# Hybrid decoder step: the first 384 tokens of the u projection from x before its norm, with the norm's inverse root applied at eviction, first weights in halves, and 48 TensorE products of zeros at the start

## The chip, the cores and the metric

The kernel runs on one core of a Trainium2 chip. The metric is the device time of one execution in microseconds (us), the median of three runs for the kernel before. The engines are TensorE (PE, with PEld for its weight loads), VectorE (DVE), ScalarE (ACT), GpSimd (POOL) and SyncE (SP), which only issues DMAs; ACT and POOL issue DMAs too.

## The reference

One layer of a decoder with three token mixers, for 1024 prompt tokens and 32 sample tokens together (1056 columns). What the change touches is the norm in front of the combined projection and the first columns of that projection, u, which feed the S5 mixer:

```python
def rmsnorm(x, w):
    xf = x.astype(jnp.float32)
    y = xf * lax.rsqrt(jnp.mean(xf * xf, axis=-1, keepdims=True) + EPS)
    return (y * w.astype(jnp.float32)).astype(x.dtype)
...
    h = rmsnorm(x, norm1_w)
    proj = h @ w_in
...
    y_b, s5_new = s5_mixer(proj[..., OFF_U:OFF_Q], ...)
```

The inverse root is one number for each token. It can be applied to h before the product, or to the product of (x times the norm's weight) behind it: the result is the same sum.

## The kernel before

Tokens lie along the free dimension, channels on the 128 partitions: x is eight tiles (k = 0 to 7) of 128 channels by 1056 tokens. The tokens are worked in three chunks, 0 and 1 of 384 and 2 of 288 columns. Every product is made of three TensorE products of 128 by 128 weights: operands are split into a high part (HH of the activations, WH of the weights) and a low part (HL, WL), and `mm3` multiplies HL by WH, HH by WL and HH by WH into one PSUM bank. Each engine runs its list of instructions in order; semaphores join them.

The u projection has four output tiles (j = 0 to 3), each with weights of 1024 columns. Units 0 and 1 of the weights go into WH and WL, units 2 and 3 into WXH and WXL. TensorE works `u_pair(j, n)`: tiles j and j+1 of chunk n, over all eight k, 48 products. The order is pairs (0, 0) and (2, 0), then the same two for chunk 1 and for chunk 2.

Ahead of each chunk stands its norm. ACT and DVE square x and DVE adds the eight squares; TensorE sums over partitions (`x_sums_pe`), ACT takes the root (`x_root_act`), DVE the reciprocal (`x_recip_dve`), and TensorE spreads it over partitions (`x_spread_pe`). Then, for each k, `x_split_dve` makes the normed row on DVE (line 702), ACT rounds it to HH (line 714), and DVE subtracts to get HL (line 691). The sums and the spread of chunks 1 and 2 are put between products of the second pair of the chunk ahead, behind k = 1 and k = 3. ACT evicts the products of u to UF (line 2398).

High parts of weights are made by ACT (lines 2355, 2344, 2348), low parts by POOL (lines 1496 and 1487). Behind chunk 2 the gates begin: `gate(0)` needs unit 4 of the weights (high part by ACT in `high_weights`, low part by POOL) in WH slot 0. `taps(0)`, two thirds into gate 0 (behind its chunks 0 and 1), needs the S5 matrices W_re and W_im, which DVE makes in six operations of 2048 columns right behind the last split of the 24. POOL makes the powers they need (`s5_powers`, `s5_rows`).

SP issues, in this order, chunk 0 of x, two small tables (HOT, RTAB), weights 0, 1 and 2, chunk 1 of x, weights 3, chunk 2 of x and the rest. ACT issues one DMA, the parameters.

Of the kernel before, what the change touches and what calls it, by code (L numbers as in the profile page):

```python
# [9 lines left out]
F32 = mybir.dt.float32  # L10
# [146 lines left out]
def build(nc, io):  # L157
# [255 lines left out]
    s_xc = [dma_sem("x_chunk1_first"), dma_sem("x_chunk1_last"), dma_sem("x_chunk2")]  # L413
# [6 lines left out]
    first_high, half_ok = sem("first_weights_high"), sem("first_weights_half_split")  # L420
    s_rawx = [dma_sem(f"weights_second_pair{i}") for i in range(2)]
# [57 lines left out]
    h_lo_pool = sem("h_low_by_pool")  # L479
# [127 lines left out]
    def x_spread_at(n):  # L607

        return bank[(4, 7, 5)[n]]

    def x_full(i):

        return bank[5 + i % 2] if i < KD else HF[i % 2]

    def x_loaded(n, k):

        return s_x[k] if n == 0 else s_xc[k // 4] if n == 1 else s_xc[2]

    def x_first_square(eng, k):

        eng.wait_ge(x_loaded(0, k), 16)
        if k % 2 == 0:
            nc.scalar.activation(x_square_at(0, k), X0[:, k, 0:384], ACT.Square).then_inc(pq_done, 1)
        else:
            nc.vector.tensor_tensor(x_square_at(0, k), X0[:, k, 0:384], X0[:, k, 0:384], ALU.mult).then_inc(pq_used, 1)

    def x_squares_act(n, ks):
        c0, w = CHUNKS[n]
        base = FIRST_ADDED + KD * (n - 1)
        for k in ks:  # L630
            nc.scalar.wait_ge(x_loaded(n, k), (16, 64, 128)[n])
            if k >= 4 or n == 2:
                nc.scalar.wait_ge(pq_used, base + k - 3)
            nc.scalar.activation(x_square_at(n, k), X0[:, k, c0:c0 + w], ACT.Square).then_inc(pq_done, 1)

    def x_add_dve(n, ks):
        dve = nc.vector
        c0, w = CHUNKS[n]
        for k in ks:
            i = FIRST_ADDED + KD * (n - 1) + k  # L640
            dve.wait_ge(pq_done, FIRST_SQUARES + KD * (n - 1) + k + 1)
            if k == 0:
                dve.tensor_copy(ACC[:, c0:c0 + w], x_square_at(n, k)).then_inc(pq_used, 1)
            else:
                dve.wait_ge(pq_used, i)
                dve.tensor_tensor(ACC[:, c0:c0 + w], ACC[:, c0:c0 + w], x_square_at(n, k), ALU.add).then_inc(pq_used, 1)

    def x_first_sums_pe():

        for k, added in ((1, 2), (3, 4), (7, FIRST_ADDED)):  # L650
            nc.tensor.wait_ge(pq_used, added)
            for j in range(3):
                last = nc.tensor.matmul(x_sums_at(0)[:, j:j + 1], x_square_at(0, k)[:, P * j:P * j + P], prm("ones", 0, 1),
                                        start=(k == 1 and j == 0), stop=k == KD - 1, skip_group_check=True)
# [3155 lines left out]
```

## Time and profile before

| | us |
|---|---|
| median of 3 runs | 1686.33 |
| lowest and highest | 1684.88, 1686.92 |
| span of the profiled execution | 1684.5 |
| TensorE busy in it | 1654.0 (98%) |
| DVE, POOL, ACT busy | 966.9, 791.2, 556.0 |
| first product of u | 17.30 |
| first product of gate 0 | 69.16 |
| first product of taps(0) | 77.89 |

TensorE works without a break from 17.30 us on but for some short waits, so its few idle pieces, and the rate of its products where the clock is low, make up what is not work. What lies between two products of one engine is read from the start of one to the start of the next, since their records overlap.

### The profile page before, as it was taken

Reading aid. Unit: us, or ns where it says so; the run is one execution under the profiler, and the core shown is the slowest. Engines: PE = TensorE matmul, PEld = TensorE weight load, DVE = VectorE, ACT = ScalarE, POOL = GpSimd, SP = SyncE. Lnnn points to the kernel's source line nnn. Section 1 sums busy time; section 2 is a strip of 40 time slices with the busy share of each in tenths; the row PEclk is TensorE's granted clock in tenths of the full one; section 3 lists DMA queues with packets and bytes.
Section 4 is the critical chain, followed back from the end, with each engine's and each line's share of the span. In section 5 each row is a group of like instructions: output and inputs, shape, how many; then the busy total and the mean of one; then the engine's idle time right before and its main releaser. Section 6 shows DMA issues by size and latency. Waiting matters only on the chain. (4 is left out here: it accounts for less than half of the span.)

```text
span 1684.5 us, 30884 instructions
## 1 busy us (share of the span) xinstructions
PE 1654.0 (98%) x12241; PEld 1604.7 (95%) x12241; DVE 966.9 (57%) x1642; ACT 556.0 (33%) x1240; POOL 791.2 (47%) x756
## 2 busy tenths in 40 slices
PE   7999999999999999999999999999999999999997
PEld 7999999999999998888899999999999999999997
DVE  6859811406634554778873289666665565744346
ACT  5332121342213332543411154443443333322233
POOL 5483122322221111141322325877777777787774
PEclk9999999999999999999999999999999999999998
DMA  5364363232233234434365431543433344966443
GB/s 209 84 127 133 104 203 98 89 92 91 87 93 103 89 130 134 161 115 140 126 218 191 152 126 42 180 162 145 151 141 141 141 167 165 367 224 267 162 187 103
DMA packets 95805, 245.85 MB, mean 146 GB/s; under 512 B 14369, under 2 KB 42273, under 8 KB 95417
## 3 DMA queue, kind: packets, MB, share of 16 engines
q1 hardware_dynamic: 73824, 174.48, 30.5%
q0 software_dynamic: 10256, 33.59, 6.7%
q10 hardware_dynamic: 11592, 35.96, 6.3%
q8 instruction: 90, 1.47, 0.4%
q14 instruction: 43, 0.34, 0.1%
HBM read 177.11 MB, written 66.65 MB: 145 GB/s over the span
## 5 line engine op out<-in xcount | busy, mean ns | idle before, releaser
L1642 PE MATMUL ps<-HL,WH 128*128 128x384 f32 (+1 forms) x1536 | 507.7, 331 | 4.4 <-DVE HL L691 1.8
L1643 PE MATMUL ps<-HH,WL 128*128 128x384 f32 (+1 forms) x1536 | 497.4, 324 | 0.0
L1644 PE MATMUL ps<-HH,WH 128*128 128x384 f32 (+1 forms) x1536 | 496.3, 323 | 0.0
L1642 PEld LDWEIGHTS ps<-HL,WH 128*128 128x128 f32 x1536 | 289.4, 188 | 15.6 <-issue 9.3
L1643 PEld LDWEIGHTS ps<-HH,WL 128*128 128x128 f32 x1536 | 289.7, 189 | 0.3
L1644 PEld LDWEIGHTS ps<-HH,WH 128*128 128x128 f32 x1536 | 289.6, 189 | 0.0
L1285 POOL TENSOR_TENSOR WL<-WRAW,WH 128x1024 fp32r<-128x1024 f32 x59 | 145.0, 2457 | 243.3 <-DMA WH<-in_w 243.3
L1282 POOL DMA_DIRECT2D WH<-in_w x59 | 34.6, 586 | 354.4 <-PE ps L1644 352.9
L2932 DVE TENSOR_TENSOR X<-X,ps 128x528 f32<-128x528 f32 (+2 forms) x170 | 107.9, 656 | 155.5 <-PE ps L2238 104.6
L2327 ACT ACTIVATE GT<-ps 128x384 f32<-128x384 f32 (+1 forms) x72 | 33.4, 465 | 215.5 <-PE ps L1644 183.5
L2932 DVE TENSOR_TENSOR RB<-RB,ps 128x528 f32<-128x528 f32 x60 | 42.1, 701 | 103.4 <-ACT RB L2847 85.9
L1310 POOL TENSOR_TENSOR WRAW<-WRAW 128x512 f32<-128x512 f32 (+2 forms) x72 | 91.8, 1275 | 9.9 <-DVE STG L2932 4.6
L1310 POOL TENSOR_TENSOR RAWB<-RAWB 128x512 f32<-128x512 f32 (+2 forms) x72 | 87.6, 1216 | 5.4
L2236 PE MATMUL ps<-HL,RINGB 128*128 128x264 f32 x272 | 77.4, 285 | 2.1 <-DVE GT L2932 2.1
L2237 PE MATMUL ps<-HH,RINGB 128*128 128x264 f32 x280 | 79.5, 284 | 0.0
L2238 PE MATMUL ps<-HH,RINGB 128*128 128x264 f32 x280 | 79.5, 284 | 0.0
L2236 PE MATMUL ps<-HL,WH 128*128 128x264 f32 x274 | 77.9, 284 | 0.3 <-issue 0.3
L2236 PE MATMUL ps<-HL,WL 128*128 128x264 f32 x270 | 76.6, 284 | 0.0
L2236 PE MATMUL ps<-SOP,RINGB 128*128 128x264 f32 x264 | 75.2, 285 | 0.0
L2237 PE MATMUL ps<-HH,WL 128*128 128x264 f32 x264 | 75.0, 284 | 0.0
L2238 PE MATMUL ps<-SOP,RINGB 128*128 128x264 f32 x264 | 74.9, 284 | 0.0
L2237 PE MATMUL ps<-SOP,RINGB 128*128 128x264 f32 x264 | 74.9, 284 | 0.0
(467 smaller groups left out, 4266.2 us busy)
## 6 DMA issues: line engine op xcount, KB each, us to landing
WRAW<-in_w SPq DMA_DIRECT2D x75, 512.0 KB, 3.4
ffn_scratch<-STG SPq DMA_DIRECT2D x70, 528.0 KB, 3.6
WH<-in_w POOLq DMA_DIRECT2D x62, 512.0 KB, 4.6
SOP<-ffn_scratch SPq DMA_DIRECT2D x36, 528.0 KB, 7.9
gate_scratch<-GT ACTq DMA_DIRECT2D x24, 528.0 KB, 3.2
PX<-gate_scratch ACTq DMA_DIRECT2D x22, 528.0 KB, 4.2
HL<-ffn_scratch SPq DMA_DIRECT2D x22, 528.0 KB, 10.4
RAWB<-in_w SPq DMA_DIRECT2D x10, 1024.0 KB, 6.2
```

The costliest lines, as they stand in the source:

```text
L1282: nc.gpsimd.dma_start(WH[:, slot, 0:wd], src[:, 0:wd]).then_inc(s_high[slot], 16)
L1285: nc.gpsimd.tensor_tensor(WL[:, slot, 0:wd], WRAW[:, slot, 0:wd], WH[:, slot, 0:wd].bitcast(F32), ALU.subtract).then_inc(split_ok, 1)
L1310: return nc.gpsimd.tensor_tensor(out, a, b, op)
L1642: nc.tensor.matmul(out, wh, rl, start=start, stop=False)
L1643: nc.tensor.matmul(out, wl, rh, start=False, stop=False)
L1644: return nc.tensor.matmul(out, wh, rh, start=False, stop=stop)
L2236: nc.tensor.matmul(out, wh, ml, start=product in FRESH and k == 0, stop=False, skip_group_check=True)
L2237: nc.tensor.matmul(out, wl, mh, start=False, stop=False, skip_group_check=True)
L2238: last = nc.tensor.matmul(out, wh, mh, start=False, stop=k == nk - 1, skip_group_check=True)
L2327: nc.scalar.activation(GT[:, c0:c0 + w], acc_of(no, n)[:, 0:w], ACT.Tanh, scale=0.5).then_inc(acc_free[n], 1)
L2932: return nc.vector.tensor_tensor(out, a, b, op)
```

## The change

- TensorE starts with 48 products of 128 by 128 zeros (IDB, which POOL clears).
- Pair (0, 0) and (2, 0) multiply x times the norm's weight, not normed: ACT makes HH from x (`x_plain_high_act`), DVE makes HL (`x_plain_low_dve`). DVE evicts these four tiles times the inverse root (`evict_first_u_dve`), which it copies from PSUM to GT.
- Chunk 0's squares (eight, all on ACT) come behind the weights' high parts; POOL adds them in three operations of 1536, 768 and 384 columns. Its sums and spread stand in pair (2, 1).
- Chunk 1's sums come behind k = 3 of pair (2, 0) (before: k = 1) and its spread behind k = 6 (before: k = 3). In pair (2, 1) the sums of chunk 2 come behind k = 4 and its spread behind k = 6. DVE adds the squares of chunks 1 and 2 in three operations of two tiles each and one of one tile, in the place of one copy and seven additions.
- The normed split of chunk 0 is still needed by the gates and all that follows. It is made last: DVE's order is chunk 1, chunk 2, chunk 0.
- Weights 0 and 1 are loaded in halves from ACT's queue, ahead of its first work; SP's queue starts with x, then weights 2 and 3, then chunk 1 of x. DVE, no longer POOL, makes the low parts of weights 0, 1 and 3.
- ACT makes the high parts of weights 4 and 5 behind the last of the 24 splits, as before; that split is now chunk 0's.

```diff
+        x_plain_high_act(0)
         high_half(0)
-        x_root_act(0)
+        for k in range(1, 4):
+            x_plain_high_act(k)
         high_half(1)
...
+        high_weights(2)
+        high_weights(3)
+        x_first_squares_act(range(KD))
+        nc.scalar.activation(SF("unused_root")[:, 0:1], ZERO[:], ACT.Sqrt)
+        x_squares_act(1, range(KD))
+        x_root_act(1)
...
+        x_split_dve(0, 5)
+        x_add_dve(2, 0)
+        x_split_dve(5, 7)
+        x_add_dve(2, 1)
+        x_split_dve(7, 8)
+        x_add_dve(2, 2)
+        x_add_dve(2, 3)
+        x_recip_dve(0)
+        x_root_copy_dve()
+        evict_first_u_dve(0)
         x_recip_dve(2)
-        x_split_dve(16, 24)
+        for j in range(1, 4):
+            evict_first_u_dve(j)
+        x_split_dve(8, 24)
...
+        pe.wait_ge(consts_ok, 2)
+        for _ in range(48):
+            nc.tensor.matmul(bank[4][:, 0:P], IDB[:], IDB[:], start=True, stop=True)
         pe.wait_ge(s_par, 16)
-        x_first_sums_pe()
-        bias_by_distance(0)
-        bias_by_distance(1)
-        x_spread_pe(0)
         u_pair(0, 0)
-        pe.wait_ge(bias_ev, 2)
-        u_pair(2, 0, {1: lambda: x_sums_pe(1), 3: lambda: x_spread_pe(1)})
+        u_pair(2, 0, {3: lambda: x_sums_pe(1), 4: lambda: bias_by_distance(0), 5: lambda: bias_by_distance(1),
+                      6: lambda: x_spread_pe(1)})
         u_pair(0, 1)
-        u_pair(2, 1, {1: lambda: x_sums_pe(2), 3: lambda: x_spread_pe(2)})
+        u_pair(2, 1, {1: lambda: x_sums_pe(0), 3: lambda: x_spread_pe(0), 4: lambda: x_sums_pe(2),
+                      6: lambda: x_spread_pe(2)})
...
-        gate(0, [0, 1])
+        gate(0, [0], lambda n, k: pe.wait_ge(h_lo, 2 * KD + k + 1))
+        gate(0, [1])
         taps(0)
```

ACT, from the high parts of weights 2 and 3 (WXH) to the root of chunk 1 (RC), before (HH rows are chunk 0's splits, BT the bias table):

```order
L2344 CAST WXH<-WXR 128x1024 [waits dma_weights_second_pair0]
L714 CAST HH<-ps 128x384 [waits h_full]
L634 ACTIVATE SQ<-X 128x384 [waits dma_x_chunk1_first] x2
L714 CAST HH<-ps 128x384 [waits h_full]
L2344 CAST WXH<-WXR 128x1024 [waits dma_weights_second_pair1]
L714 CAST HH<-ps 128x384 [waits h_full]
L2361 COPY BT<-ps 8x264 [waits bias_product]
L714 CAST HH<-ps 128x384 [waits h_full]
L2361 COPY BT<-ps 8x264 [waits bias_product]
L714 CAST HH<-ps 128x384 [waits h_full]
L634 ACTIVATE SQ<-X 128x384 [waits x_square_added,dma_x_chunk1_last] x4
L669 ACTIVATE RC<-ps,PRM 128x3 [waits norm_chunk_sum_done]
```

The same stretch of ACT now (UF holds chunk 0's squares for a time):

```order
L2369 CAST WXH<-WXR 128x1024 [waits dma_weights_second_pair0]
L2369 CAST WXH<-WXR 128x1024 [waits dma_weights_second_pair1]
L640 ACTIVATE UF<-X 128x384 x8
L2448 ACT_TABLE_LOAD
L2448 ACTIVATE SP<-ZERO 128x1
L661 ACTIVATE SQ<-X 128x384 [waits dma_x_chunk1] x4
L661 ACTIVATE SQ<-X 128x384 [waits x_square_added,dma_x_chunk1] x4
L695 ACTIVATE RC<-ps,PRM 128x3 [waits norm_chunk_sum_done]
```

Four of chunk 1's eight squares stood between the casts; now all eight stand behind both casts, behind chunk 0's eight squares and behind a table load.

ACT, from the evictions of chunk 1 of u to the high parts of weights 4 and 5 (WH), before:

```order
L2398 COPY UF<-ps 128x3x8x16 [waits acc_done1] x2
L714 CAST HH<-HF 128x288 [waits h_full] x8
L2398 COPY UF<-ps 128x3x8x16 [waits acc_done1] x2
L2398 COPY UF<-ps 128x2x8x16 [waits acc_done2]
L2400 COPY UF<-ps 128x32
L2453 DMA u_scratch<-UF 128x1056 [waits acc_free2]
L2398 COPY UF<-ps 128x2x8x16 [waits acc_done2]
L2400 COPY UF<-ps 128x32
L2348 CAST WH<-WRAW 128x1024 [waits acc_done2,dma_weights0]
L2348 CAST WH<-WRAW 128x1024 [waits acc_done2,dma_weights1]
```

And now:

```order
L757 CAST HH<-HF 128x288 [waits h_full] x4
L757 CAST HH<-HF 128x384 [waits h_full] x2
L2423 COPY UF<-ps 128x2x8x16 [waits acc_done2]
L2425 COPY UF<-ps 128x32
L2423 COPY UF<-ps 128x2x8x16 [waits acc_done2]
L2425 COPY UF<-ps 128x32
L757 CAST HH<-HF 128x384 [waits h_full] x6
L2481 DMA u_scratch<-UF 128x1056 [waits acc_free2,acc_free0]
L2373 CAST WH<-WRAW 128x1024 [waits acc_done2,dma_weights0]
L2373 CAST WH<-WRAW 128x1024 [waits acc_done2,dma_weights1]
```

The eight splits of chunk 0 (128x384) now stand behind chunk 2's and ahead of the high parts of weights 4 and 5.

DVE, from the reciprocal of the last root to the first operation of W_re, before:

```order
L677 RECIPROCAL RC<-RC 32x1
L702 SCALAR_TENSOR_TENSOR HF<-X,PRM,ps 128x288 [waits norm_chunk_rstd_spread] x2
L691 TENSOR_TENSOR HL<-HF,HH 128x288 [waits h_high]
...
L691 TENSOR_TENSOR HL<-HF,HH 128x288 [waits h_high] x2
L2932 TENSOR_TENSOR W_re<-PWD,BC 128x2048 [waits s5_rows_ready]
```

And now, with the evictions of chunk 0 of u (UF) ahead and chunk 0's splits (from GT) behind:

```order
L703 RECIPROCAL RC<-RC 32x1
L723 TENSOR_TENSOR UF<-ps,GT 128x3x8x16 [waits acc_done0,first_rstd_copied] x3
L745 SCALAR_TENSOR_TENSOR HF<-X,PRM,ps 128x288 [waits h_low,norm_chunk_rstd_spread] x2
L730 TENSOR_TENSOR HL<-HF,HH 128x288 [waits h_high]
...
L745 SCALAR_TENSOR_TENSOR HF<-X,PRM,GT 128x384 [waits h_low,acc_done0,first_rstd_copied]
L730 TENSOR_TENSOR HL<-HF,HH 128x384 [waits h_high] x2
L2960 TENSOR_TENSOR W_re<-PWD,BC 128x2048 [waits s5_rows_ready]
```

Eight more splits of 384 columns and three evictions stand ahead of W_re.

## Rows read from the trace of the kernel before

**Rows 1.** The page: engines' busy time; then who TensorE waited for, whole span.
```profile
PE 1654.0 (98%) x12241; PEld 1604.7 (95%) x12241; DVE 966.9 (57%) x1642; ACT 556.0 (33%) x1240; POOL 791.2 (47%) x756
...
PE ps L653 <- DVE SQ L2932: 6.2, 1, 6.2
PE ps L2236 <- DVE GT L2932: 2.1, 1, 2.1
```

**Rows 2.** Timeline of TensorE, 0 to 30 us: start, duration, engine, line, operation.
```profile
17.30 0.69 PE L1642 MATMUL ps<-HL,WH 128*128 128x384 f32 x1 [1.82 <-DVE HL L691]
...
20.67 0.52 PE L1643 MATMUL ps<-HH,WL 128*128 128x384 f32 x1
20.99 0.38 PE L1644 MATMUL ps<-HH,WH 128*128 128x384 f32 x1
...
27.51 0.34 PE L1642 MATMUL ps<-HL,WXH 128*128 128x384 f32 x1
...
28.56 0.34 PE L1642 MATMUL ps<-HL,WXH 128*128 128x384 f32 x1
```

**Rows 3.** Timeline of TensorE, 66 to 78 us: last product of u, gate 0, taps.
```profile
68.73 0.29 PE L1644 MATMUL ps<-HH,WXH 128*128 128x288 f32 x1
69.16 0.41 PE L1642 MATMUL ps<-HL,WH 128*128 128x384 f32 x1
...
77.89 0.41 PE L1793 MATMUL ps<-CDG,W_re 128*128 128x32 f32 x2
```

**Rows 4.** Timelines of DVE and ACT, 4 to 13 us, with waits for DMAs.
```profile
4.71 0.56 DVE L625 TENSOR_TENSOR SQ<-X 128x384 f32<-128x384 f32 x1 [4.71 <-DMA X<-in_x]
...
7.90 0.52 ACT L623 ACTIVATE HF<-X 128x384 f32<-128x384 f32 x1 [0.52 <-DMA X<-in_x]
...
12.79 0.62 ACT L2355 CAST WH<-WRAW 128x512 fp32r<-128x512 f32 x1 [0.62 <-DMA WRAW<-in_w]
```

**Rows 5.** Timeline of ACT, 13 to 33 us: casts, squares, a table load.
```profile
13.47 1.12 ACT L2355 CAST WH<-WRAW 128x512 fp32r<-128x512 f32 x2
...
18.38 1.05 ACT L2344 CAST WXH<-WXR 128x1024 fp32r<-128x1024 f32 x1
...
19.70 0.95 ACT L634 ACTIVATE SQ<-X 128x384 f32<-128x384 f32 x2
...
31.12 1.28 ACT L2430 ACT_TABLE_LOAD   x1
```

**Rows 6.** Timeline of DVE: one addition; chunk 1's splits; chunk 2's splits.
```profile
9.88 0.56 DVE L2932 TENSOR_TENSOR HF<-HF,ACC 128x384 f32<-128x384 f32 x1
...
33.70 1.14 DVE L702 SCALAR_TENSOR_TENSOR HF<-X,PRM,ps 128x384 f32<-128x384 f32 x2 [2.25 <-PE ps L683]
...
35.55 0.61 DVE L702 SCALAR_TENSOR_TENSOR HF<-X,PRM,ps 128x384 f32<-128x384 f32 x1
...
40.32 0.61 DVE L702 SCALAR_TENSOR_TENSOR HF<-X,PRM,ps 128x384 f32<-128x384 f32 x1
...
42.13 1.32 DVE L691 TENSOR_TENSOR HL<-HF,HH 128x384 fp32r<-128x384 f32 x2
...
51.94 0.94 DVE L702 SCALAR_TENSOR_TENSOR HF<-X,PRM,ps 128x288 f32<-128x288 f32 x2 [2.41 <-PE ps L683]
```

**Rows 7.** Timeline of DVE, 59 to 78 us: the six operations of W.
```profile
59.84 2.28 DVE L2932 TENSOR_TENSOR W_re<-PWD,BC 128x2048 f32<-128x2048 f32 x1
...
64.36 2.29 DVE L2932 TENSOR_TENSOR W_re<-W_re,KTS 128x2048 f32<-128x2048 f32 x1
66.69 4.36 DVE L2932 TENSOR_TENSOR W_im<-PWD,BC 128x2048 f32<-128x2048 f32 x1
...
75.48 2.29 DVE L2932 TENSOR_TENSOR W_im<-W_im,KTS 128x2048 f32<-128x2048 f32 x1
```

**Rows 8.** Timeline of POOL: low parts of weights 2 and 3, then of 4 and 5.
```profile
19.51 4.93 POOL L1487 TENSOR_TENSOR WXL<-WXR,WXH 128x1024 fp32r<-128x1024 f32 x2 [2.31 <-ACT WXH L2344]
...
64.66 4.24 POOL L1487 TENSOR_TENSOR WL<-WRAW,WH 128x1024 fp32r<-128x1024 f32 x1 [9.78 <-ACT WH L2348]
...
69.66 3.64 POOL L1487 TENSOR_TENSOR WL<-WRAW,WH 128x1024 fp32r<-128x1024 f32 x1
```

**Rows 9.** Timeline of TensorE, 48 to 52 us: sums and spread among products.
```profile
48.20 0.65 PE L661 MATMUL ps<-PRM,ACC 128*128 128x1 f32 x6
...
50.97 0.94 PE L683 MATMUL ps<-PRM,RC 128*128 128x128 f32 x6
```

More of the change, by code:

```diff
@@ L615, in x_loaded, with x_plain_high_act @@
     def x_loaded(n, k):
[L617 to L625, printed above, removed]
+        return s_x[k] if n == 0 else s_xc[n]
+    def x_plain_high_act(k):
+        nc.scalar.wait_ge(s_x[k], 16)
+        if k == 0:
+            nc.scalar.wait_ge(s_par, 16)
+        nc.scalar.mul(HH[:, k, 0:384], X0[:, k, 0:384], prm("norm1", k, 1)).then_inc(xp_hi, 1)
@@ L634, in x_squares_act, with x_add_dve @@
             nc.scalar.activation(x_square_at(n, k), X0[:, k, c0:c0 + w], ACT.Square).then_inc(pq_done, 1)
-    def x_add_dve(n, ks):
+    def x_add_dve(n, i):
         dve = nc.vector
         c0, w = CHUNKS[n]
[L639 to L654, printed above, removed]
-        last.then_inc(pn_sum, 1)
-    def x_sums_pe(n):
-        nc.tensor.wait_ge(pq_used, FIRST_ADDED + KD * n)
+        added, squares = 4 * (n - 1), KD * n
@@ new lines, in x_add_dve @@
+        if i < 3:
+            dve.wait_ge(pq_done, squares + 4 + 2 * i)
+        if i >= 1:
+            dve.wait_ge(pq_used, added + i)
+        if i < 3:
+            dve.tensor_tensor(SQ[:, 0:2, 0:w], SQ[:, 0:2, 0:w], SQ[:, 2:4, 0:w], ALU.add).then_inc(pq_used, 1)
+        else:
+            dve.tensor_tensor(ACC[:, c0:c0 + w], SQ[:, 0, 0:w], SQ[:, 1, 0:w], ALU.add).then_inc(pq_used, 1)
+    def x_sums_pe(n):
+        if n == 0:
+            nc.tensor.wait_ge(x0_add, 3)
+            nc.tensor.wait_ge(acc_free[1], 1)
+        else:
+            nc.tensor.wait_ge(pq_used, 4 * n)
+        if n == 2:
+            nc.tensor.wait_ge(acc_free[1], 2)
@@ L1675, in unit, with gate @@
                 tile(args[0], slot, *args[1:], **kw)
-        def gate(g, chunks=range(3)):
+        def gate(g, chunks=range(3), before=None):
             u = (UNIT0["gates1"] + g) if g < 12 else (UNIT0["gates2"] + g - 12)
             no = (TILE0["gates1"] + g) if g < 12 else (TILE0["gates2"] + g - 12)
-            unit(u, u % 2, [((no, 0, KD, HH, HL), dict(chunks=chunks))])
+            unit(u, u % 2, [((no, 0, KD, HH, HL), dict(chunks=chunks, before=before))])
         def simple_loop(name, pairs, nk, RH, RL, skip=0, kbase=0, before=None):
@@ L2332, in _ @@
         act.dma_start(PRM[:, 0:NPAR_FIRST], io["params"][:, 0:NPAR_FIRST]).then_inc(s_par, 16)
+        for half in range(2):
+            c = slice(512 * half, 512 * half + 512)
+            for u in range(2):
+                act.dma_start(WRAW[:, u, c], io["w"][u][:, c]).then_inc(s_half0 if half == 0 else s_raw[u], 16)
         act.wait_ge(consts_ok, 1)
```

273 lines of the change are left out of this document (144 added, 129 removed).

## Prediction

> **What bounds the kernel now.** I read the page's busy times first, then the list of who TensorE waited for, then the timelines of the first 80 us, since nothing behind taps(0) is changed. TensorE is busy 98% of the span, and its two largest waits are 6.2 us at the very start and 2.1 us far behind [rows 1]. So the time moves by what TensorE gains or loses in the first 80 us and by nothing else. Today its first product of u starts at 17.30. Up to 20.99 products of 384 columns start 0.32 us apart (1.2 GHz), then 0.175 us apart (six of them, one k of a pair, in 1.05: 27.51 to 28.56; 2.4 GHz) [rows 2]. From there it works through u until 68.73, gate 0 at 69.16 and taps(0) at 77.89 [rows 3]. Taps(0) needs W_re and W_im, and DVE ends the last of its six operations at 75.48 + 2.29 = 77.77 [rows 7]: taps(0) starts 0.1 us behind it. So two chains meet at 77.8 with no slack between them: TensorE's own work, and DVE's: 24 splits, then 17.9 us of W (59.84 to 77.77). The change makes the first start earlier and the second longer. The question is where DVE ends.
>
> **The gain at the start.** ACT's four loads of half weights share the transfer engines with x. Parameters and two tiles of x, some 600 KB, were in at 4.71, and some 1560 KB (seven tiles) at 7.90 [rows 4]. In the new order the first halves are in when 1300 to 1450 KB are: 7.0 to 7.5 us, I take 7.3. Then two casts, 1.1 us [rows 5], and DVE's low parts behind them, about 0.7 each (0.56 for 384 columns [rows 6], 2.28 for 2048 [rows 7], so 0.16 plus 1.03 ns a column): first product at 9.3, 8.0 us earlier than now. If the zeros leave the clock high, pair (0, 0) takes 8 x 1.05 = 8.4; if not, 12 products at 0.32 make it 1.7 longer. So it ends at 17.7 to 19.4.
>
> **Where it is lost first: chunk 1's sums.** ACT is a queue, and I add it from 7.3. Spacing of starts [rows 5]: casts of 512 columns 0.50, of 1024 about 0.95, squares or products of 384 columns 0.42, a table load 1.28. Four half casts 2.0, seven products of x with the weight 2.9 (the first is done before 7.3), exp, sin and cos 0.3, a table 1.3, the casts of weights 2 and 3 1.9, chunk 0's squares 3.4, a table and its dummy 1.4: together 13.2, so 20.5. Then chunk 1: four squares to 22.3, three additions of 768 columns (0.96 each by the line above) with two rounds of two squares (0.95) between them, because buffers 2 and 3 are reused, and a last addition of 0.56: 27.7. POOL adds chunk 0's squares from about 19.4 for over 6 us (2.46 for 1024 columns [rows 8]), beside DVE's first two additions. W_im's first operation took 4.36 in the place of 2.29 beside POOL's subtraction of 4.24 [rows 7, 8], while the DVE addition beside small POOL work took 0.56 [rows 6]. So this costs between 0 and 1.8; I take 1.0, near the middle, since POOL's operation here is as wide as there but has no broadcast operand beside it: 28.7.
>
> TensorE cannot use the wait. Pair (2, 0) starts when both low parts of weights 2 and 3 are there. The high parts end at 15.8; DVE's 1.2 and POOL's 2.46 run side by side, so 18.3, up to 19.5 if they hinder each other. Behind k = 3 (4.2 us) TensorE stands at 22.5 to 23.7, in front of the sums. It waits there for 5 to 6 us. All of the earlier waits (zeros or not, the low parts of weights 2 and 3) are covered by this one and cost nothing; if it did not exist they would cost 0 to 3 us.
>
> The Trainium skill (GPSIMD Engine Reference, Specifications) says that GpSimd's SBUF interfaces are shared with VectorE and that they collide with VectorE instructions of two SBUF inputs. The trace agrees for W_im's first operation (4.36), not for the one ahead of it (W_re's last, 2.29, beside the same POOL operation, which itself grew from 2.46 to 4.24) [rows 7, 8]. By the rule alone the additions would take the whole 1.8, and the sum would be 0.8 higher.
>
> **Then the spread, the splits and the second loss.** Behind the sums (0.35, half of the six in [rows 9]) TensorE must do k = 4, 5 and 6 before the spread. It stood idle for over 5 us, so I take the rate that it had at 17.30: 12 products at 0.32, six at 0.175, 4.9 us in the place of 3.15. With two bias products and the spread, 0.8, that is 34.8. Before, these splits began at 33.70 [rows 6]: the whole head start is gone and 1.1 more.
>
> The Trainium skill (TensorE: Matmul & The Clock Gate, What's actually happening) says that the array falls back to half rate when it has been idle. No row of this trace shows an idle piece as long behind a warm one; without the rule's effect the sum would be 1.75 lower.
>
> Chunk 1's eight splits take 33.70 to 43.45, 9.75 us [rows 6]. Two additions of 576 columns (0.75 each) now stand among them, with some 0.6 of waits for ACT's squares: 2.1, so 46.7. Pair (0, 1) is paced by them; its last k ends at 47.8. The spread of chunk 2 comes behind seven k of pair (2, 1), 7.35, and behind two sums and two spreads, 1.5: 56.7. Before, chunk 2's splits began at 51.94 [rows 6]; now 56.8, 4.9 later.
>
> Chunk 2's splits take 7.9 (51.94 to 59.84 [rows 6, 7]). Then comes what was first before and is now last: chunk 0's eight splits, at 1.19 each (35.55 to 40.32 is four [rows 6]), 9.5 us. DVE starts W_re at 56.8 + 7.9 + 9.5 = 74.2 in the place of 59.84, **14.4 us later**. The six operations take 17.9 again, since POOL's two low parts (weights 4 and 5, 4.24 and 3.64 [rows 8]) fall beside them again: ACT casts these weights behind the last split. W_im is ready at 92.1.
>
> **Is TensorE there first?** ACT's last split at 73.6, a DMA issue of 0.4, a cast of 1.06: 75.1. POOL's low part 2.46 to 4.24 [rows 8]: gate 0 starts at 77.6 to 79.3 (before 69.16). Its first two chunks take 77.89 - 69.16 = 8.7 [rows 3], up to 1.7 more with the low clock: at taps(0) at 86.3 to 89.7. DVE is last, by 2.4 to 5.8 us. So gate 0's own delay is hidden, and the loss is that of DVE. Behind taps(0) all is in the old order and TensorE has no idle time in which to catch up [rows 1]. Sum: 1684.5 + 14.4 = 1698.9 for the profiled execution. The median of the runs is 1.8 above its span: **1700.7 us**.
>
> What has one answer: the 48 zeros, 5 us at the low rate, lie in time in which TensorE waits for weights anyway. The evictions by DVE (four of about 0.56) lie between the root and the spread of chunk 2, where DVE waits for TensorE; their last could cost 0.3. POOL's powers start at 26 to 28 (before 32.9) and are not waited for. Chunk 1 of x is in when some 5330 KB are: at the 300 KB a us between the two landings above, at 20.5, just when ACT asks for it.
>
> **Ends of the range.** Down: no collision of the additions 1.0, no low clock behind the sums 1.8, W without a collision up to 4.3 but then TensorE is last at 88 to 90, so 3 at most: together 5.8, 1695. Up: collisions 0.8 in the additions and some 2 in W, a low clock behind the wait for W 1.7, half weights 0.5 later (each us of theirs moves all of ACT's queue): 5, 1706.
>
> **The rivals.** *The sums are in time.* If ACT and DVE brought chunk 1's squares to TensorE by 23, the wait at k = 3 and the low clock would go, and the spread would come at 27, 7.8 earlier. Then W would be ready at 84.3, and the time would be 1693. For it: ACT spends over half its queue on work that is not chunk 1's. Against: 13.2 us of queue stand ahead, all from measured spacings.
>
> *The head start is kept (faster).* DVE is idle 43% of the span [rows 1], and if the new work all lay in that idle time, so that the 24th split ended by 59.8 less 8, TensorE would run through from 9.3 with the first 12 products at full rate: 8.0 to 9.7 saved, 1677 to 1679. The point from which it decides is the start of W_re: before 59.8 there is a gain, behind it a loss of as much. Against it: between the first and last split DVE has 24 splits and two rounds of additions, over 30 us, and its start is bound to the spread, which TensorE reaches only behind its seventh k; W_re before 59.8 would need the first split before 20, when chunk 1's squares are not begun. Half of this gives no change, about 1686.
>
> **How the numbers follow.** Forecast, 1695 to 1706: 0.77. Sums in time or other partial gains, 1688 to 1695: 0.08. Faster: 0.07. No change: 0.04. Over 1706: 0.04. The range 1692 to 1706 holds some 0.82. About 0.2%, 3.4 us, is what a measurement of this kernel can tell from no change: faster 0.07, same 0.04, slower 0.89.
>
> **What would show it.** TensorE's list of waits has one of 5 to 6 us at the sums (line 687) near 23 to 29, one of 6 to 8 at gate 0 for POOL's low part, and one of 2 to 6 at taps(0) for DVE. The first product of u is at 9 to 9.5, the first split of chunk 1 at 33 to 35, W_re at 72 to 76. Products behind the sums start 0.32 apart for a while. I am wrong if W_re starts before 65, or if TensorE has no wait over 1 us at the sums.

## The result and the profile after

| | before | after |
|---|---|---|
| median, us | 1686.03 (1684.88 to 1686.92, 4 runs) | 1712.80 (1712.36 to 1715.77, 4 runs) |
| span of the profiled execution | 1684.5 | 1714.1 |
| first product of u | 17.30 | 8.90 |
| chunk 1's first split | 33.70 | 40.79 |
| chunk 2's first split | 51.94 | 64.91 |
| W_re begins | 59.84 | 82.54 |
| gate 0 begins | 69.16 | 87.23 |
| taps(0) begins | 77.89 | 100.53 |

The changed kernel takes 1.0164 of the time before, 95% interval 1.0149 to 1.0178: 26.8 us slower. The profiled execution is the slowest of its four, and the other three have spans of 1710.7 to 1711.4.

The page of the changed kernel, its line of busy times. The list behind it says whom TensorE waited for: sum, times, longest.

```profile
PE 1671.2 (97%) x12277; PEld 1616.4 (94%) x12277; DVE 972.1 (57%) x1643; ACT 558.4 (33%) x1247; POOL 786.6 (46%) x755
```

Its list of waits:

```profile
PE ps L1662 <- issue: 6.3, 1, 6.3
PE ps L687 <- DVE ACC L675: 5.8, 1, 5.8
PE ps L1815 <- DVEq L3038: 3.1, 1, 3.1
PE ps L1662 <- DVE WL L2960: 2.9, 1, 2.9
```

Against [rows 1], TensorE has three long waits that it did not have: for the sums of chunk 1 (5.8), for gate 0 (6.3, line 1662) and for taps(0) (3.1, line 1815). It is also busy for 17 us more with only 36 products more in its records (12277 against 12241), and the 48 zeros are busy for only 4.85 of that: many products ran at half rate.

TensorE's timeline, the changed kernel: the zeros and the first product; the sums and what follows; gate 0; taps(0). It answers to [rows 2, 3, 9].

```profile
1.16 4.85 PE L1797 MATMUL ps<-IDB 128*128 128x128 bf16 x48 [1.16 <-POOL IDB L1306]
8.90 0.66 PE L1662 MATMUL ps<-HL,WH 128*128 128x384 f32 x1 [2.89 <-DVE WL L2960]
...
29.52 1.44 PE L687 MATMUL ps<-PRM,ACC 128*128 128x1 f32 x6 [5.75 <-DVE ACC L675]
...
32.57 0.52 PE L1664 MATMUL ps<-HH,WXH 128*128 128x384 f32 x1
33.02 1.05 PE L1765 MATMUL ps<-HOT,RTAB 33*8 33x264 f32 x2
33.99 0.69 PE L1662 MATMUL ps<-HL,WXH 128*128 128x384 f32 x1
...
39.27 1.48 PE L709 MATMUL ps<-PRM,RC 128*128 128x128 f32 x6
...
87.23 0.66 PE L1662 MATMUL ps<-HL,WH 128*128 128x384 f32 x1 [6.33 <-issue]
...
100.53 0.41 PE L1815 MATMUL ps<-CDG,W_re 128*128 128x32 f32 x2 [3.05 <-DVEq L3038]
...
108.73 0.30 PE L1815 MATMUL ps<-CDG,W_re 128*128 128x32 f32 x2
```

Six sums take 1.44 in the place of 0.65, six spreads 1.48 in the place of 0.94. From the first product of taps(0) to that of taps(1) it is 8.20 (100.53 to 108.73). In the kernel before, the same two stand at 77.89 and 82.97, 5.08 apart.

Busy time of each engine in stretches of the changed kernel. The third number from the end is the clock granted to TensorE, then come the DMA share and GB/s.

```profile
26.00:30.00 4.00, 0.48 (x3) 0.48 (x3) 2.37 (x3) 0.94 (x2) 3.67 (x9) 0.50 0.04 15
38.00:42.00 4.00, 4.00 (x16) 4.00 (x16) 1.15 (x3) 0.56 (x2) 3.69 (x11) 0.50 0.00 0
42.00:46.00 4.00, 3.70 (x19) 2.91 (x18) 3.69 (x7) 2.81 (x8) 3.74 (x5) 0.88 0.01 2
...
104.00:108.00 4.00, 4.00 (x19) 4.00 (x19) 3.97 (x2) 0.00 (x0) 0.00 (x0) 0.53 1.28 111
108.00:112.00 4.00, 4.00 (x32) 4.00 (x32) 3.97 (x3) 1.46 (x2) 1.00 (x1) 1.00 1.25 180
```

The clock is at 1.2 GHz from 26 us until behind 42, and again from 101 until near 108. A third low stretch, 84 to 91 us, lies around the start of gate 0 and is hidden, since TensorE waits for DVE behind it. In the kernel before the products run at the full rate from 21 us on through all three places.

DVE's timeline of the changed kernel: chunk 1's additions, the first splits of the three chunks, the first three operations of W. It answers to [rows 6, 7].

```profile
23.17 1.20 DVE L673 TENSOR_TENSOR SQ<-SQ 128x768 f32<-128x768 f32 x1 [3.74 <-ACT SQ L661]
25.43 1.42 DVE L673 TENSOR_TENSOR SQ<-SQ 128x768 f32<-128x768 f32 x1 [1.06 <-ACT SQ L661]
27.91 0.96 DVE L673 TENSOR_TENSOR SQ<-SQ 128x768 f32<-128x768 f32 x1 [1.06 <-ACT SQ L661]
...
40.79 1.14 DVE L745 SCALAR_TENSOR_TENSOR HF<-X,PRM,ps 128x384 f32<-128x384 f32 x2 [9.32 <-PE ps L709]
...
64.91 0.94 DVE L745 SCALAR_TENSOR_TENSOR HF<-X,PRM,ps 128x288 f32<-128x288 f32 x2 [1.04 <-PE ps L709]
...
72.43 0.62 DVE L745 SCALAR_TENSOR_TENSOR HF<-X,PRM,GT 128x384 f32<-128x384 f32 x1
...
82.54 2.28 DVE L2960 TENSOR_TENSOR W_re<-PWD,BC 128x2048 f32<-128x2048 f32 x1
84.74 4.43 DVE L2960 TENSOR_TENSOR KTS<-PWD,BC 128x2048 f32<-128x2048 f32 x1
89.20 4.36 DVE L2960 TENSOR_TENSOR W_re<-W_re,KTS 128x2048 f32<-128x2048 f32 x1
```

POOL's timeline in the same place, answering to [rows 8]:

```profile
83.15 3.88 POOL L1505 TENSOR_TENSOR WL<-WRAW,WH 128x1024 fp32r<-128x1024 f32 x1 [35.95 <-ACT WH L2373]
...
87.54 3.88 POOL L1505 TENSOR_TENSOR WL<-WRAW,WH 128x1024 fp32r<-128x1024 f32 x1
```

DVE waited 9.3 us for the spread of chunk 1. Chunk 0's splits begin at 72.43 and W_re at 82.54. In W the two engines seem to take turns. POOL's first subtraction starts in the middle of a DVE operation that ends at 84.82, and ends 2.2 us behind that (2.4 to 2.5 is its time alone [rows 8]). DVE's next one (2.28 alone) ends 2.1 us behind POOL's end at 87.03, and so on. The operation of DVE that had begun before POOL's still took 2.28. DVE loses the rest of POOL's operation each time.

### The profile page after: what moved, and what is told of

It is laid out like the page before. It is cut to its first block and busy times, and to the rows that moved or that the text cites. A ratio compares the mean times of both kernels' runs of the same rounds, so it can differ in the third digit from the quotient of the medians.

```text
span 1714.1 us, 30960 instructions
## 1 busy us (share of the span) xinstructions
PE 1671.2 (97%) x12277; PEld 1616.4 (94%) x12277; DVE 972.1 (57%) x1643; ACT 558.4 (33%) x1247; POOL 786.6 (46%) x755
## 3 DMA queue, kind: packets, MB, share of 16 engines
q8 instruction: 91, 1.49, 0.4%
## 5 line engine op out<-in xcount | busy, mean ns | idle before, releaser
L1662 PEld LDWEIGHTS ps<-HL,WH 128*128 128x128 f32 x1536 | 290.8, 189 | 29.5 <-issue 20.4
```

The lines of the kernel that those rows point to most:

```text
L1662: nc.tensor.matmul(out, wh, rl, start=start, stop=False)
```

## The experiments

They ran in three groups, each beside runs of the kernel before (medians 1685.13, 1685.88, 1686.64), so a kernel is given as its distance from the kernel before of its own group. That distance was 26.8 for the changed kernel. A ratio's interval is some 0.0016 to either side, 2.7 us: smaller differences are read from the traces, by the start of the same instruction. There is one trace for each kernel.

**No zeros.**

```diff
-        for _ in range(48):
-            nc.tensor.matmul(bank[4][:, 0:P], IDB[:], IDB[:], start=True, stop=True)
```

> The changed kernel without its 48 products of zeros. Theory (they lie in time in which TensorE waits for weights, and their clock is lost again in the 2.9 us before the first product of u; what they could save is covered by the wait for chunk 1's sums): no change against the changed kernel, 1712.8 within 2 us, sums of chunk 1 still at 29.5. Rival (they keep the clock up for the first pair and that counts): 1 to 3 us slower.

Measured: 1711.47 (+26.3, ratio 1.0152, 1.0135 to 1.0169). First product at 10.12, sums at 30.27, chunk 1's first split at 41.55, W_re at 83.28. The zeros are worth nothing where they stand: in the changed kernel they end 2.9 us before the first product, the first eleven products start 0.32 apart in spite of them, and the wait for the sums swallows what is left.

Eleven traces have these same 48 zeros ahead of the same first product, and they don't agree. The combined kernel with long zeros, described below, starts like this:

```profile
1.16 5.30 PE L1799 MATMUL ps<-IDB 128*128 128x128 bf16 x48 [1.16 <-POOL IDB L1306]
8.81 0.41 PE L1662 MATMUL ps<-HL,WH 128*128 128x384 f32 x1 [2.34 <-DVE WL L2965]
...
18.94 0.44 PE L1662 MATMUL ps<-HL,WXH 128*128 128x384 f32 x1 [1.49 <-POOLq L1517]
```

Here the products run at the full rate from the first one on, and also behind the wait of 1.49. Over the eleven traces, the clock stayed up behind idle pieces of 2.31 and 2.34 us, it was low for 3.4 us behind pieces of 2.57 to 3.02, and for 6.8 us behind pieces of 3.37 to 3.62. Why the zeros ended at another time in each trace no run shows.

**Zeros in the wait for the sums.** TensorE works off 96 products of zeros while it waits.

```diff
-        u_pair(2, 0, {3: lambda: x_sums_pe(1), ...
+        u_pair(2, 0, {3: lambda: (fill(bank[4], 96), x_sums_pe(1)), ...
```

> The changed kernel with 96 more products of zeros (5.3 us at the high rate) ahead of the wait for chunk 1's sums, behind k = 3 of pair (2, 0). Theory (the idle 5.8 us drop TensorE's clock to 1.2 GHz, and k = 4 to 6, which stand ahead of the spread, are paid at it): no product behind the sums at 0.32 us spacing, the first split of chunk 1 at about 35 in the place of 40.8, and the time 5 to 7 us lower, 1706 to 1708. Rival (the low rate comes from the small float32 products between, not from the idle time): the rate stays low and the time changes by less than 1.5 us.

Measured: 1707.48 (+22.4, ratio 1.0130, 1.0113 to 1.0147). TensorE's timeline, the zeros and what follows:

```profile
23.12 5.53 PE L1799 MATMUL ps<-IDB 128*128 128x128 bf16 x96
29.03 0.83 PE L687 MATMUL ps<-PRM,ACC 128*128 128x1 f32 x6 [0.37 <-DVE ACC L675]
29.72 0.42 PE L1662 MATMUL ps<-HL,WXH 128*128 128x384 f32 x1
29.98 0.34 PE L1663 MATMUL ps<-HH,WXL 128*128 128x384 f32 x1
```

The sums wait for DVE as before (29.03), but what follows runs at the full rate, and chunk 1's first split is at 35.30: 6.3 us behind the sums in the place of 11.3. So the low clock cost 5.0 us there. W_re stands at 77.48, 5.1 earlier. The rival (the small float32 products lower the rate, not the idle time) is out: they are all still there.

**Chunk 1's squares ahead of chunk 0's.** ACT computes the squares that are needed first, first; POOL's additions wait for all 16.

```diff
-        x_first_squares_act(range(KD))
         nc.scalar.activation(SF("unused_root")[:, 0:1], ZERO[:], ACT.Sqrt)
         x_squares_act(1, range(KD))
+        x_first_squares_act(range(KD))
```

> The changed kernel with chunk 1's squares ahead of chunk 0's on ACT (POOL adds chunk 0's behind all sixteen). Theory (ACT's queue sets when the sums come; the clock holds in an idle time of 2.5 us): sums at about 26 in the place of 29.5, high rate behind them, first split of chunk 1 at 31 in the place of 40.8; 9 to 10 us lower, about 1703. Rival (the queue order alone counts, the clock falls all the same): 3 to 4 us lower, 1709. Rival (DVE is not what sets the time of W): no change.

Measured: 1706.51 (+21.4, ratio 1.0124, 1.0108 to 1.0141). The sums stand at 25.53, with a wait of 1.26, and yet TensorE's timeline shows:

```profile
27.44 0.61 PE L1765 MATMUL ps<-HOT,RTAB 33*8 33x264 f32 x2
27.98 0.60 PE L1662 MATMUL ps<-HL,WXH 128*128 128x384 f32 x1
28.38 0.52 PE L1663 MATMUL ps<-HH,WXL 128*128 128x384 f32 x1
```

The products behind the sums start 0.175 apart until 27.4, then 0.32 apart until 34.7, although TensorE is at work throughout. The theory that the clock holds in such a wait failed. The clock fell some two microseconds behind a wait of only 1.3 us, but the small sums and bias products stand there too, and this run doesn't tell whether the wait would have been enough without them. So of the 9.0 us that the earlier sums (4.0) and a high clock (5.0) would give together, 6.1 came: the first split is at 34.69.

**No normed split of chunk 0.** Gate 0 and all behind it read the unnormed x of the first 384 tokens.

```diff
-        x_split_dve(8, 24)
+        x_split_dve(8, 16)
```

> The changed kernel without the normed split of chunk 0 (16 DVE operations, 8 ACT casts left out; all that follows reads chunk 0's un-normed rows). Theory (DVE is last at taps(0), and these splits stand ahead of W_re and of the high parts of weights 4): W_re starts at about 72.8 in the place of 82.5, gate 0 at 77.5, and the time is 9 to 11 us lower, about 1703. Rival (TensorE's own chain sets the time, DVE only a little behind): at most 3 us lower, the length of the wait at taps(0).

Measured: 1703.77 (+18.6, ratio 1.0108, 1.0091 to 1.0125). W_re at 72.91 in the place of 82.54, taps(0) at 90.84 in the place of 100.53. At W_re the second split costs what its DVE time is, 9.6 us. By the medians it is 8.2, each of the two distances known to some 2.7.

**The spread earlier.** The bias products go ahead of the sums, the spread stands behind k = 4.

```diff
-        u_pair(2, 0, {3: lambda: x_sums_pe(1), 4: lambda: bias_by_distance(0), 5: lambda: bias_by_distance(1),
-                      6: lambda: x_spread_pe(1)})
+        u_pair(2, 0, {1: lambda: bias_by_distance(0), 2: lambda: bias_by_distance(1), 3: lambda: x_sums_pe(1),
+                      4: lambda: x_spread_pe(1)})
```

> The spread of chunk 1 stands behind k = 4 in the place of k = 6, and the two bias products stand ahead of the sums, in the time in which TensorE waits. In the changed kernel 11.3 us lie between the sums (29.52) and the first split (40.79): four k at the low clock less the last, two bias products and their restarts. My theory (what costs is all that stands between the sums and the spread, since it runs at the low clock): sums near 29.5, spread near 32.8, first split near 34. TensorE then has k = 5, 6, 7 at the low clock and reaches pair (0, 1) near 38, DVE's eight splits end near 47, pair (0, 1) near 48 in the place of 54.4, so 6 to 7 us less at the start of chunk 2's splits (near 58.5 in the place of 64.9) and at W: about 1706. Rival (only the clock counts, and the products would be late anyway): the first split moves but the second set of splits stays within 2 us of 64.9, about 1711.

Measured: 1706.35 (+20.5, ratio 1.0117, 1.0102 to 1.0133). Sums at 29.20, first split at 34.10, chunk 2's first split at 57.90, W_re at 75.53, 7.0 earlier. The low clock is still there (0.50 from 28 to 36), but less stands between the sums and the spread, and it ended at 36.7, where that of the changed kernel ended at 42.9.

**Zeros in all three waits**, with 48 and then with 86 ahead of taps(0).

```diff
+        fill(bank[6], 96)
         gate(0, [0], lambda n, k: pe.wait_ge(h_lo, 2 * KD + k + 1))
         gate(0, [1])
+        fill(bank[6], 48)
         taps(0)
```

> Products of zeros in all three waits: 96 ahead of the sums of chunk 1, 96 ahead of gate 0 and 48 ahead of taps(0). With those ahead of the sums alone the time was 1707.5, and behind the wait for taps(0) the clock was low for some 3.5 us (98 to 101.5). Theory: the zeros ahead of taps(0) keep the clock up and save 1.3 to 1.7 us of that, those ahead of gate 0 save nothing since TensorE waits for DVE behind it anyway: about 1706. Rival (the low clock behind taps(0) costs nothing at the end): 1707.5.

> The kernel with products of zeros in all three waits, now with 86 in the place of 48 ahead of taps(0). With 48 the zeros ended 2.1 us ahead of taps(0), and the clock was low from 96 to 103 us. Theory (the clock falls since TensorE stands idle for those 2.1 us, however warm it was): zeros that reach up to taps(0) keep it at the full rate, and give back the half of those 7 us: about 1704.3. Rival (the small products of taps(0), 32 columns each, let it fall, or the zeros don't count): 1707.8 as with 48.

Measured: 1707.82 with 48 (+21.9, ratio 1.0124, 1.0109 to 1.0140) and 1706.26 with 86 (+19.6, ratio 1.0108, 1.0092 to 1.0125). The first of the two expectations failed: 48 products of zeros ended 2.1 us ahead of taps(0), and the clock was low behind it, longer than without them. With 86 there is no idle piece and no low clock. A stretch of the kernel with 48, the clock ahead of the DMA share:

```profile
96.00:98.00 2.00, 2.00 (x11) 2.00 (x11) 2.00 (x2) 0.00 (x0) 0.00 (x0) 0.50 1.27 120
```

and one of the kernel with 86:

```profile
98.00:104.00 6.00, 6.00 (x48) 6.00 (x47) 5.97 (x3) 1.46 (x2) 0.57 (x1) 1.00 1.20 151
```

From the first product of taps(0) to that of taps(1), the traces of all 14 kernels fall into three groups:

| | us | kernels |
|---|---|---|
| clock high | 5.07 to 5.08 | before, before with zeros, 86 zeros, combined with long zeros |
| low for some 3 us | 6.59 to 6.64 | no zeros, zeros ahead of the sums, chunk 1 first, no split, copy by POOL |
| low for some 6.5 us | 8.17 to 8.52 | changed, early spread, 48 zeros, combined, combined without split |

The low clock costs 1.5 or 3.1 to 3.4 us there, and the length of the wait (1.4 to 7.3 us) doesn't tell which: 8.17 came behind the shortest. The medians of the two kernels of this experiment differ by less than their intervals; the 3.15 us are from the traces.

**A copy in the place of POOL's subtraction.** The low parts of weights 4 and 5 are copies of the weights, so gates 0 and 1 are not computed as in the reference.

```diff
+            if u in (4, 5):
+                nc.gpsimd.tensor_copy(wl, WRAW[:, u % 2, :]).then_inc(split_ok, 1)
+                return
```

> The changed kernel, with the low parts of weights 4 and 5 not computed by GpSimd's subtraction of two tiles but replaced by a copy of one tile, so the numbers of gates 0 and 1 are not those of the reference. Theory (an operation of DVE with two SBUF inputs that meets GpSimd's subtraction ends only when that ends: two of the six operations of W take 4.4 in the place of 2.3): with a copy all six take 2.3, W_im is ready at 96.1 in the place of 100.4, TensorE comes to taps(0) at about the same time and has no wait there and no low clock behind it: 4.3 us and about 3 us less than now, 1705 to 1706. Rival (the two operations are slow for the DMA traffic or the PSUM work beside them): W takes 17.9 as now, 1712.

Measured: 1709.21 (+22.6, ratio 1.0138, 1.0116 to 1.0160). DVE's timeline:

```profile
84.39 3.12 DVE L2963 TENSOR_TENSOR KTS<-PWD,BC 128x2048 f32<-128x2048 f32 x1
87.55 3.01 DVE L2963 TENSOR_TENSOR W_re<-W_re,KTS 128x2048 f32<-128x2048 f32 x1
```

and POOL's:

```profile
82.78 2.59 POOL L1506 CAST WL<-WRAW 128x1024 fp32r<-128x1024 f32 x1 [35.95 <-ACT WH L2376]
...
85.88 2.53 POOL L1506 CAST WL<-WRAW 128x1024 fp32r<-128x1024 f32 x1
```

The two slow operations shrink from 4.43 and 4.36 to 3.12 and 3.01, not to 2.3 as expected. Both again end 2.1 to 2.2 us behind the end of POOL's (85.37 and 88.41). So it is POOL's operation that holds them up, and a copy does so too; it costs less (1.5 us together in the place of 4.2) since it is not held up by DVE itself and so ends earlier. The rival, DMA traffic or PSUM, would have left the two at 4.4. W_im was ready at 97.4, and taps(0) started at 97.53, 3.0 earlier (W_re had begun 0.35 earlier), behind a wait of 1.8: the time fell by 4.2 us, not by the 7 expected.

**Together**: chunk 1's squares first, bias products and spread early, the spread of chunk 2 behind k = 3 in the place of 6, zeros in the waits (20 ahead of the sums, 40 ahead of gate 0, 24 ahead of taps(0)), the casts of weights 4 and 5 among the last splits. Two lines of the whole edit:

```diff
-        u_pair(2, 1, {1: lambda: x_sums_pe(0), 3: lambda: x_spread_pe(0), 4: lambda: x_sums_pe(2),
-                      6: lambda: x_spread_pe(2)})
+        u_pair(2, 1, {1: lambda: (x_sums_pe(0), x_sums_pe(2)), 2: lambda: x_spread_pe(0), 3: lambda: x_spread_pe(2)})
...
+        high_weights(4)
+        high_weights(5)
         x_split_act(18, 24)
```

> The changed kernel with the repairs that the runs point to, together: chunk 1's squares ahead of chunk 0's on ACT, bias products ahead of the sums, spread of chunk 1 behind k = 4, sums of chunks 0 and 2 both behind k = 1 of pair (2, 1) and their spreads behind k = 2 and 3, the casts of weights 4 and 5 ahead of the last splits, products of zeros ahead of the sums, of gate 0 and of taps(0). By my theory the chain is: sums 25.5, first split 28.5, eight splits and two rounds of additions to 41, pair (0, 1) to 42, chunk 2's first split near 49 (64.9 in the changed kernel, 51.9 before), 7.9 and 9.5 us of splits, W_re near 66.5, W_im ready near 84.3: 6.5 us behind the kernel before, and 1692 to 1696, I say 1694. What is left over before is then chunk 0's second split (9.5 us) less the head start. Rival (the twelve or so us of head start are all recovered once the waits are gone): 1686 or less.

Measured: 1700.24 (+14.4, ratio 1.0086, 1.0071 to 1.0102), against 1694 expected. The first splits of chunks 1 and 2 are at 29.29 and 51.18, near what was expected, but W_re is at 73.26, not at 66.5. The casts cost 4.2 of that, as the next run shows by putting them back. DVE's timeline:

```profile
68.17 0.62 DVE L745 SCALAR_TENSOR_TENSOR HF<-X,PRM,GT 128x384 f32<-128x384 f32 x1
68.71 2.75 DVE L730 TENSOR_TENSOR HL<-HF,HH 128x384 fp32r<-128x384 f32 x1
```

and POOL's:

```profile
68.26 2.78 POOL L1505 TENSOR_TENSOR WL<-WRAW,WH 128x1024 fp32r<-128x1024 f32 x1
```

DVE's subtraction of 384 columns, 0.55 elsewhere, took 2.75: it ended at 71.46, 0.4 behind POOL's (71.04). Another took 1.51 beside POOL's first, and came behind a wait of 1.2 for ACT, which had the two casts to make. In return no operation of W took over 2.29. With 24 products of zeros ahead of taps(0) TensorE still stood idle for 7.3 us, and the clock was low until 94.6.

**Together, with the casts put back and long zeros.**

```diff
-        fill(bank[6], 40)
+        fill(bank[6], 80)
...
-        fill(bank[6], 24)
+        fill(bank[6], 88)
```

> The combined kernel with the casts of weights 4 and 5 back behind the last split, and 80 and 88 products of zeros ahead of gate 0 and of taps(0) in the place of 40 and 24. With the casts among the splits, GpSimd's two subtractions met two of DVE's low parts (1.51 and 2.75 in the place of 0.55), and W_re started at 73.3 in the place of 68.3, but W then took 13.7 in the place of 17.9. TensorE stood idle for 7.3 us ahead of taps(0), and the clock was low from 87 to 94.6 behind it. Now W_re at 68.3, W_im ready near 86.1 (0.8 less), and, if the zeros reach up to taps(0), 3.8 us less for the clock: about 1695.6. If the zeros do nothing there: 1699.4.

Measured: 1696.65 (+10.0, ratio 1.0058, 1.0041 to 1.0075). W_re at 69.08, taps(0) at 87.09, and the windows show the clock high from 84 on:

```profile
84.00:90.00 6.00, 6.00 (x83) 6.00 (x81) 5.56 (x4) 0.00 (x0) 0.00 (x0) 1.00 1.27 104
90.00:96.00 6.00, 6.00 (x46) 6.00 (x45) 5.93 (x4) 1.46 (x2) 1.58 (x1) 1.00 1.28 108
```

This is the best form of the change that was found among those that compute the reference, and it is 9.2 us behind the kernel before at taps(0).

**Together, without the second split.** The same without chunk 0's normed split: gate 0 and what follows read unnormed x there. No zeros ahead of gate 0 and taps(0).

> The combined kernel without chunk 0's normed split (gate 0 and all behind it read the unnormed x of the first 384 tokens, so the output is not the reference's), with the casts of weights 4 and 5 where the changed kernel has them, and zeros ahead of u and of the sums alone. It shows what the early start is worth if the second split of chunk 0 cost nothing. In the combined kernel chunk 2's splits ended at 58.7, before at 59.84, and TensorE ended u near 67.7 (68.7 before). So W_re starts at 58.7, W_im is ready at 76.6, TensorE has no wait at taps(0), and of 8 us of head start 1 us is left: about 1684.9. Rival (the head start comes through once the second split is gone): 1678 to 1680.

Measured: 1690.64 (10 runs, 1687.97 to 1694.21; +4.0, ratio 1.0022, 1.0012 to 1.0032). TensorE's timeline at taps(0):

```profile
78.41 0.41 PE L1818 MATMUL ps<-CDG,W_re 128*128 128x32 f32 x2 [1.39 <-DVEq L3044]
```

and the stretch behind it:

```profile
80.00:86.00 6.00, 6.00 (x27) 6.00 (x27) 5.96 (x3) 0.00 (x0) 0.00 (x0) 0.50 1.28 106
```

W_re begins at 60.45, 0.6 behind the kernel before, not 1.1 ahead. TensorE comes to taps(0) at 77.0, 0.9 us before the kernel before does, waits 1.4 us and then loses 3.1 more to the low clock. So even with the second split for nothing, less than one of the 8.3 us of head start is left at taps(0), and the wait for W takes that too. This trace is of the slowest of the ten executions (1694.21): it is 3.6 us behind the kernel before at taps(1), and 3.1 more near 700 us, around a wait of 3.2 for DVE's SB (0.2 in the kernel before). Over the ten, the granted clock of the whole span runs from 0.990, here, to 0.995, the kernel before's, in the two quickest, so the low stretches are not the same in each execution.

**The kernel before, with zeros ahead of u.**

```diff
+        fill(8)
         x_spread_pe(0)
+        fill(16)
         u_pair(0, 0)
```

> The kernel before, with 8 products of zeros ahead of its first spread and 16 behind it, in the 0.9 and 1.8 us in which TensorE waits there. Its first 12 products of u start 0.32 apart (17.30 to 20.99). If the zeros give the clock back, the products are at full rate by the first or second k and pair (0, 0) is then paced by DVE's splits of 1.19 us: 0.5 to 1.0 us less, about 1685.2, hardly more than can be measured. If such zeros do nothing for the clock: 1686.0.

Measured: 1687.01 (11 runs), ratio 1.0005, 0.9996 to 1.0014: no change. The clock did come up, as TensorE's timeline shows,

```profile
17.20 0.45 PE L1643 MATMUL ps<-HL,WH 128*128 128x384 f32 x1 [0.60 <-DVE HL L691]
17.48 0.34 PE L1644 MATMUL ps<-HH,WL 128*128 128x384 f32 x1
17.66 0.33 PE L1645 MATMUL ps<-HH,WH 128*128 128x384 f32 x1
```

but W_re moved by 0.11 us (59.73) and taps(0) by as much (77.78): the low clock at the start of u was hidden behind DVE's splits.

## Why the prediction was wrong

The direction was right, and so was the chain: TensorE loses by DVE's late W, and DVE is late since the spread of chunk 1 is late and chunk 0's split comes last. The size was not: 14.4 us were forecast, 26.8 measured, and the time lies above the range.

**Right.** The first product (9.3 forecast, 8.90 measured); the wait at the sums (5 to 6, 5.75); what DVE's additions lose beside POOL's (1.0, 0.7); the wait at gate 0 (6 to 8, 6.33) hidden by the one at taps(0) (2.4 to 5.8, 3.05); the last two splits together (17.4, 17.63); W (17.9, 17.87), again with two slow operations, though now the second and third. The price of the second split (9.5) is confirmed by leaving it out (9.6).

**The step that failed** is the one behind the sums: "It stood idle for over 5 us, so I take the rate that it had at 17.30: 12 products at 0.32, six at 0.175, 4.9 us in the place of 3.15. With two bias products and the spread, 0.8, that is 34.8." It put the first split 6.1 us behind the sums; it was 11.3. With zeros in the wait it was 6.3, which divides the error. The low clock cost 5.0 in the place of 1.75: I took its length from the start of u in the kernel before [rows 2], 3.7 us, and here it lasted from 26 us to behind 42. The small products cost 2.0 more than counted, at the full clock already: with the zeros the 6.3 us are 3.15 of large products and 3.1 of sums, bias products and spread, where I had 1.15. From the product ahead of two of bias to the one behind them it is 0.8 at the full clock (1.42 at the low one, 32.57 to 33.99), twice, where I had 0.8 for both and the spread. What ends a low stretch stays open. At the start of u it ended within 3.7 us of dense products; behind the sums, with bias products and spread among the large ones, it took 13.4 us (29.5 to 42.9). With the bias products ahead of the sums it took 7.5 (29.2 to 36.7), but that run moved the spread too, and with chunk 1 first the low stretch was 7 us although they stood in their old place. So no run tells the two apart.

**Terms that were off**, from TensorE's and DVE's starts. Forecast 14.4. Sums at 29.5 in the place of 28.7: 0.8. The cause is ACT's queue. It began at 6.79 (7.3 forecast), but its seven products of x with the weight took 3.6 where I had 2.9, and it waited 0.4 for weights, so chunk 1's first square stands at 21.39 in the place of 20.5:

```profile
10.89 2.13 ACT L628 ACTIVATE HH<-X,PRM 128x384 fp32r<-128x384 f32 x4
...
21.39 1.75 ACT L661 ACTIVATE SQ<-X 128x384 f32<-128x384 f32 x4
```

DVE's additions beside POOL's (1.20 and 1.42 in the place of 0.96) cost no more than forecast. Sums to first split: 5.2. First split of chunk 1 to that of chunk 2, 24.1 in the place of 22.0: 2.1, of which 1.6 is sums and spreads of chunks 0 and 2 that take 0.72, 0.83, 0.65 and 0.94 where I had 1.5 for all four. The last splits: 0.2. That makes W_re late by 22.7, as measured. Behind taps(0) the low clock, taken at nothing with a bound of 1.7, cost 3.1. From 122 us (25.8 behind) to 1057 us (27.5 behind) 1.7 us were added, 1.0 of it one wait for DVE's PX that grew from 0.8 to 1.8; why it grew is open. Together 27.5, against 26.8 between the medians. The profiled execution lost 2 more behind 1057 us, 1.5 of it near 1478 us in two waits for DVE's X (0.78 and 0.87) where the kernel before has one of 0.34. The other executions have no trace; their spans are 2.7 to 3.4 shorter, so these late losses are likely the profiled one's own.

**The range** failed at its upper end for the same reason. I added 1.7 for a low clock at taps(0) and nothing for a longer one at the sums, though the sums' idle piece was longer than any behind which a row of the trace showed the clock. An unknown cost whose only row is from another place needs a bound above that row.

**The rivals.** *The sums are in time* (1693): with chunk 1's squares first they came at 25.5, but the clock fell all the same, 1706.5. With all repairs and W_re at 69.1 it was 1696.65. *The head start is kept* (1677 to 1679): against it stands the kernel without a second split, at 1690.64. In the trace of the combined kernel with long zeros TensorE begins u 8.5 us before the kernel before and ends it 1.15 before (67.58 and 68.73). The rest went into waits of 4.0 us (1.5 for low parts, 0.75 at the spread, 1.7 for DVE's splits), 1.3 of zeros, and 2 of bias products, sums and spread of chunk 0 that the kernel before does while it waits for weights, and the changed one among products.

The Trainium skill (TensorE: Matmul & The Clock Gate, What's actually happening) says that the array falls back to half rate when it has been idle. The trace agrees at all three waits of the changed kernel (5.75, 6.33 and 3.05 us). Behind nine shorter ones (1.27 to 1.49 us) in four other kernels the clock stayed up. The Trainium skill (GPSIMD Engine Reference, Specifications) says that GpSimd's SBUF interfaces are shared with VectorE and collide with VectorE instructions of two SBUF inputs. The traces agree: DVE's subtraction took 2.75 in the place of 0.55, and two operations of W 4.4. Ahead of the result I held that W_re's last operation in the kernel before (2.29 beside POOL's) speaks against it. It doesn't: it had begun before POOL's, and it was POOL's that grew [rows 7, 8].

## What to carry to other kernels

Starting the bottleneck engine earlier is worth nothing unless every engine that feeds it comes earlier too: work out the start of the last producer first (here DVE's W_re) and look at the head start last. Where TensorE will stand idle for some microseconds, put the work behind the wait at half rate into the upper bound until a trace shows otherwise, or fill the wait up to the very instruction that ends it. For a wait of one to two microseconds these runs show both outcomes. Small products that filled a wait are dear once they stand among large ones.

## What the runs showed of the hardware

- The clock fell behind idle pieces of 1.26 us (chunk 1 first) and 1.39 us (combined without split), in the first case 2 us after work had begun again, and the low stretch then lasted about 7 us. In the changed kernel it lasted 17 us (26 to 43), around a wait of 5.75. But nine pieces of 1.27 to 1.49 us left it high: with zeros ahead of the sums (1.32, 1.34), with 48 zeros at taps(0) (1.43, 1.32, 1.33), with 86 (1.33, 1.35), combined with long zeros (1.49, 1.27). Large products stood behind all nine, small ones behind or soon behind the two others; no run tests whether that decides.
- Products of zeros that reached up to taps(0) kept the clock (86: 5.07 between taps(0) and taps(1)), 48 that ended 2.1 us early did not (8.22). A gap does not always lose it: the 48 at the program's start kept it over gaps of 2.31 and 2.34 us in two traces and lost it in the nine with longer ones, and the 80 ahead of gate 0 kept it over 1.27.
- Between taps(0) and taps(1) there were only three lengths in 14 kernels: 5.1, 6.6 and 8.2 to 8.5.
- DVE and POOL took turns on SBUF tiles, as the ends show: an operation with two SBUF inputs that starts beside the other engine's ends about its own time behind the other's end, and one already under way is not slowed. DVE with 2048 columns 4.43 (84.74 to 89.17, POOL's end 87.03), with 384 columns 2.75 (to 71.46, POOL's end 71.04); POOL with 1024 columns 3.88 (to 87.03, DVE's end 84.82). DVE's additions of 768 columns, 0.96 alone, fit too: they ended 0.8 us behind POOL's. That such an operation does not start at all before the other has ended is my reading of these ends; no run tested it apart.
- The granted clock of the kernel before reads 1.00 from 16 to 20 us, though its products start 0.32 apart there, and 0.175 apart with zeros ahead. Its trace holds no record of the clock ahead of 21.06 us, and a stretch without a record reads as 1.00. The distance between starts is the surer sign.
